# Peeling the tail of a feed-forward loop and moving a row scale behind the matmuls in a two-block transformer kernel

## The chip, the cores and the metric

The kernel runs on one core of one Trainium2 chip. The metric is the device time of one execution in microseconds (us), as the median of several runs. All times below are in us unless marked ns.

## The reference

The program computes two transformer blocks, one after the other, for one sequence of 256 tokens and a model width of 2048, in float32. Cut to what the change touches:

```
first block:   x = x + gt1 * (merged @ w_out)
               h = modulate(rms_norm(x, g_ffn), sh2, sc2)
               a = causal_dwconv(h @ w_gate, conv_w, conv_b)        # hidden width 5632
               y = (silu(a) * (h @ w_up)) @ w_down
               x = x + gt2 * y
               x = rms_norm(x, g_final)
second block:  h = rms_norm(x, norm_g)                              # EPS = 1e-6 in both norms
               q, k, v, r, a_lr = split(h @ gla_w_in)               # gated linear attention
               x = x + gla(...) @ gla_w_out
               g, u = split(rms_norm(x, norm_g2) @ w_gu)
               x = x + (silu(g) * u) @ w_down
```

`gt2` is a row of 2048 numbers made from `c @ w_ada`. Between the two blocks stand two RMS norms in a row, `g_final` and `norm_g`, and each needs the mean square of whole token rows.

## The kernel before, in words

**Tiling.** The 256 tokens are two blocks of 128 partitions (`TB = 2`). Every large product streams its weight through a ring of four 1 MB slabs (`raw`): 512 rows by 512 columns, read by the DMA queue of SyncE (SP). A slab is two halves. For each half ScalarE (ACT) rounds the weight into `whi`, VectorE (DVE) makes the remainder `wlo = raw - whi`, and TensorE (PE) does 12 matmuls of 128x512: two row tiles by two token blocks by three products (hi*hi, lo*hi, hi*lo). This stands in `split` on ACT and DVE and in `half` on PE. The ring holds four halves, so `split` of half n waits until PE has used half n-4, and ACT and DVE run at most four halves ahead of PE.

**Order.** Each engine's program is one list, written out by hand. `body(it, phase, per, hooks)` walks over the halves, calls `split` for each, and after half idx runs the steps that `hooks` has for idx. Whatever a step waits for holds up all later splits of that engine. A group of halves accumulates into one of two pairs of PSUM banks, `lin[0]` and `lin[1]` (one bank for each token block), which alternate; ACT drains token block 0 and counts `free0`, DVE drains block 1 and counts `free1`.

**The feed-forward part.** The hidden width 5632 is 11 blocks of 512 (`FB = 11`). Phase `F1p` makes gate and up of block 0 (16 halves). Phase `F1` is a hardware loop over ten iterations of 24 halves: gate of block j+1 (8), down of block j (8: four output column blocks c of 2 halves each), up of block j+1 (8). PE transposes the up values at idx 1 (`turn_up`) and the gate values at idx 9 (`turn_gate`); DVE does the convolution (`conv`, after splits 14 and 16), `activate` (18) and `hidden` (5), which makes `hid_hi` and `hid_lo`, the operand of the down product. The results of each down block are added to `yacc`: token block 1 by DVE, block 0 through `dstage` by GpSimd (POOL). Phase `F1e` is the down product of block 10 alone (8 halves). PE has nothing else to do there, so it waits for `turn_up` and `hidden`. During `F1e` the row `gt_row` is made (`modulation_row(1)`, from PE's `ada_rows(3)`), and `combine` adds `yacc * gt_row` to X, one column block after the other.

**Between the blocks.** After the last `combine`, DVE makes `xs = X * gfin` (2 instructions of 128x2048), ACT sums the squares of X and xs (4 of 128x2048), DVE and ACT form the scale `ry` of each token, xs is multiplied by it, PE transposes xs (`first_features`, then four more turns inside the first group of phase `GQ`), ACT multiplies by the column `g_n0` into `aff`, and DVE makes `act_hi` and `act_lo`. Meanwhile POOL scales X itself in place with `rstd` and `gfin`. Phases `GQ`, `GV`, `GR` then read these features. Phases `F2p`, `F2`, `F2e` of the second block have the same form as F1, without convolution and without `gt_row`; their result is added to X directly and written out in four DMAs.

Of the kernel before, what the change touches and what calls it, by code (L numbers as in the profile page):

```python
# [33 lines left out]
GL_ITEMS = (1, 2, 0, 3, 4, 5, 6)  # L34

# [4 lines left out]
    ("F1p", 1, 16, 2), ("F1", FB - 1, 24, 6), ("F1e", 1, 8, 4),  # L40
    ("GQ", 2, 16, 2), ("GV", 2, 16, 2), ("GR", 2, 16, 2), ("GO", 2, 16, 2),
    ("F2p", 1, 16, 2), ("F2", FB - 1, 24, 6), ("F2e", 1, 8, 4),
# [11 lines left out]
for _n in range(108):  # L54
    _at = 4 + _n if _n < 64 else 8 + _n if _n < 96 else 20 + _n if _n < 102 else (124, 125, 126, 126, 127, 127)[_n - 102]
    CHUNKS_AT.setdefault(_at, []).append(_n)
# [7 lines left out]
def build_program(nc, A, out):  # L64
# [68 lines left out]
    dstage = at("dstage", [P, 2, NB], ARENA + 65 * KB)  # L133

# [11 lines left out]
    alrT = at("alrT", [GR, S], ARENA + 44 * KB)  # L146
    wa2 = at("wa2", [GR, GH * GK], CONST + 10 * KB + 512)
# [27 lines left out]
    par3 = at("par3", [P, 96], CONST + 6 * KB)  # L175
# [31 lines left out]
    conv_w1, conv_w2, gla_b = par3[:, 0:44], par3[:, 44:88], par3[:, 88:96]  # L207
# [32 lines left out]
    def _(sp):  # L240
# [8 lines left out]
        def ada_chunk(n, kt=None, half=None):  # L249
# [16 lines left out]
            (2, 0, rows(A["conv_w"][0, 1])), (2, 44, rows(A["conv_w"][0, 2])), (2, 88, rows(A["gla_b_a_2"][0])),  # L266
        ]
# [56 lines left out]
        def ffn(n):  # L324
# [46 lines left out]
        for c in range(4):  # L371
            sp.wait_ge(free1, 2 + G0["F2e"] + c + 1)
            sp.wait_ge(sem("dstage_free"), 2 + 4 * (2 * FB - 1) + c + 1)
# [4 lines left out]
    def _(pe):  # L378
# [14 lines left out]
        def group(it, phase, per, gper, idx0, gi, n, hooks, kt0=0, x_hi=hi, x_lo=lo, lead=None, parts=None):  # L393
# [4 lines left out]
            for i in range(n):  # L398
# [6 lines left out]
                if lead is not None and i < 4:  # L405
                    turn(lead, 4 + i)
# [39 lines left out]
        pe.wait_ge(sem("par_in"), 13 * 16)  # L446
        for n, rws in enumerate((112, 120, 96)):
# [172 lines left out]
        def ffn(n):  # L620
# [16 lines left out]
            def turn_gate(j):  # L637
                g = G0[name + "p"] + (3 if isinstance(j, int) else 6 * j - 1)
# [25 lines left out]
            with pe.Fori(0, FB - 1) as it:  # L664
# [4 lines left out]
            turn_up(FB - 1)  # L669

            def rows_now(idx):

                if idx == 1 and n == 0:
                    pe.wait_ge(sem("gpad_made"), FB)
                    ada_rows(3)
            down(0, name + "e", 8, 4, 0, 0, FB - 1, rows_now)
# [5 lines left out]
        pe.wait_ge(sem("gt_made"), 2)  # L682


        pe.wait_ge(sem("xs_made"), 6)
        first_features(xs)
# [15 lines left out]

        def turn_block(b):
# [10 lines left out]
        group(0, "GQ", 16, 2, 0, 0, 8, none, lead=xs)  # L714
        project_ranks()
        group(0, "GQ", 16, 2, 8, 1, 8, lambda idx: turn_block(0) if idx == 13 else None)
# [86 lines left out]
        pe.wait_ge(sem("xs_made"), 8)  # L803
# [5 lines left out]
    def _(act):  # L809
        pairs, affine, squared = [0], [0], [0]  # L810
# [44 lines left out]

        def features(phase, plain, scale=None, shift=None):
# [170 lines left out]
        def ffn(n):  # L1027
# [20 lines left out]
            def sigmoid(j):  # L1048
# [3 lines left out]
                else:  # L1052
                    g = G0[name + "p"] + (3 if isinstance(j, int) else 6 * j - 1)
# [24 lines left out]
            with act.Fori(0, FB - 1) as it:  # L1078
                body(it, name, 24, hooks(it, name, 6, it + 1, 27))
            hid_high(FB - 1)  # L1080
            hk = {5 + 2 * c - (c == 3 and n == 0): [lambda c=c: down(0, name + "e", 4, c, c, 2 * c + 2)] for c in range(4)}
            if n == 0:
                body(0, name + "e", 8, hk)
            else:

                for idx in range(4, 8):
                    split(0, name + "e", 8, idx)
                    for step in hk.get(idx, ()):
                        step()
                for idx in (9, 11):  # L1090
                    hk[idx][0]()
# [865 lines left out]
```

## Time and profile before

| what | value |
|---|---|
| median of 3 runs | 2992.65 us (2988.68 to 2993.77) |
| the profiled execution, its own time | 2992.77 us |
| its span in the trace | 2990.8 us |
| PE busy (matmul) | 2749.4 us, 92% of the span |
| DVE busy | 1850.3 us, 62% |
| ACT busy | 1291.7 us, 43% |
| POOL busy | 303.6 us, 10% |
| DMA | 585.39 MB, mean 196 GB/s |

The span is the time from the first to the last instruction of the trace; the run's own time is 2.0 us longer. "Busy" is the union of an engine's instructions. The granted clock of PE is shown per stretch as a share of full speed: 1.00 is 2.4 GHz and 0.50 is 1.2 GHz. Phase F1 ends and phase GQ begins at about 1665 to 1767 us in the span, F2e at 2954 us.

### The profile page before, as it was taken

To read this page: it belongs to the slowest core of one execution; us is meant where nothing else is said; L and a number is where in the kernel's file an instruction comes from. 1 tells how busy PE (TensorE), PEld (TensorE's weight loads), DVE (VectorE), ACT (ScalarE), POOL (GpSimd) and SP (SyncE) were. 2 spreads that over 40 slices of the span, in tenths; PEclk is the share of its full clock that TensorE was granted. 3 is DMA by queue.
4 is the path that set the end of the run, shared out by engine and by line. 5 is a ranking of instruction groups with operands and counts; after the bars stand their busy time and mean duration, and the time that the engine had idled before them with its cause. 6 is when DMAs were issued, how large, how long until landed. Compare 5 with 4: busy or idle time off the path is not lost. (4 is left out here: it accounts for less than half of the span.)

```text
span 2990.8 us, 34105 instructions
## 1 busy us (share of the span) xinstructions
PE 2749.4 (92%) x12279; PEld 2248.6 (75%) x12279; DVE 1850.3 (62%) x1936; ACT 1291.7 (43%) x1505; POOL 303.6 (10%) x214
## 2 busy tenths in 40 slices
PE   0699999999998999999999679998989999999998
PEld 0587888777787788888887567785678888888886
DVE  7656776677766666666666664557545555555554
ACT  1334554345444444444444343443344444444443
POOL 0000000100010111111111330004000111111112
PEclk9989999999999999999999889998999999999999
DMA  9667776656856766666555425551054555555553
GB/s 393 239 217 247 253 254 241 231 191 216 298 170 209 248 201 199 196 201 201 198 187 195 136 93 174 170 189 65 30 195 155 193 187 196 185 194 189 189 189 120
DMA packets 266917, 585.39 MB, mean 196 GB/s; under 512 B 14300, under 2 KB 16676, under 8 KB 263900
## 3 DMA queue, kind: packets, MB, share of 16 engines
q1 hardware_dynamic: 266844, 584.41, 57.6%
q8 instruction: 46, 0.75, 0.1%
q14 instruction: 27, 0.22, 0.0%
HBM read 582.26 MB, written 2.11 MB: 195 GB/s over the span
## 5 line engine op out<-in xcount | busy, mean ns | idle before, releaser
L1205 DVE TENSOR_TENSOR sb_wlo<-sb_raw,sb_whi 128x1024 fp32r<-128x1024 f32 x896 | 1106.4, 1237 | 940.3 <-ACT sb_whi L817 940.0
L817 ACT ACTIVATE sb_whi<-sb_raw 128x1024 fp32r<-128x1024 f32 x896 | 948.1, 1060 | 1416.6 <-PE lin L390 1290.6
L388 PE MATMUL lin<-sb_whi,sb_act_hi 128*128 128x512 f32 x2880 | 1147.9, 399 | 43.1 <-DVE sb_act_lo L1267 12.8
L389 PE MATMUL lin<-sb_wlo,sb_act_hi 128*128 128x512 f32 x2880 | 1131.7, 393 | 0.0
L390 PE MATMUL lin<-sb_whi,sb_act_lo 128*128 128x512 f32 x2880 | 1131.6, 393 | 0.0
L388 PEld LDWEIGHTS lin<-sb_whi,sb_act_hi 128*128 128x128 f32 x2880 | 548.1, 190 | 164.6 <-DVE sb_wlo L1205 25.2
L390 PEld LDWEIGHTS lin<-sb_whi,sb_act_lo 128*128 128x128 f32 x2880 | 547.1, 190 | 116.6
L389 PEld LDWEIGHTS lin<-sb_wlo,sb_act_hi 128*128 128x128 f32 x2880 | 548.2, 190 | 110.9 <-issue 0.2
L388 PE MATMUL lin<-sb_whi,sb_hid_hi 128*128 128x512 f32 x704 | 278.7, 396 | 6.3 <-DVE sb_hid_lo L1504 3.7
L389 PE MATMUL lin<-sb_wlo,sb_hid_hi 128*128 128x512 f32 x704 | 276.1, 392 | 0.0
L390 PE MATMUL lin<-sb_whi,sb_hid_lo 128*128 128x512 f32 x704 | 275.8, 392 | 0.0
L388 PEld LDWEIGHTS lin<-sb_whi,sb_hid_hi 128*128 128x128 f32 x704 | 133.4, 190 | 37.8 <-DVE sb_hid_lo L1504 4.1
L390 PEld LDWEIGHTS lin<-sb_whi,sb_hid_lo 128*128 128x128 f32 x704 | 133.4, 190 | 28.0
L389 PEld LDWEIGHTS lin<-sb_wlo,sb_hid_hi 128*128 128x128 f32 x704 | 133.5, 190 | 27.4 <-issue 0.2
L1849 POOL TENSOR_TENSOR sb_yacc<-sb_yacc,sb_dstage 128x512 f32<-128x512 f32 x44 | 83.4, 1894 | 691.1 <-ACT sb_dstage L831 691.1
L1849 POOL TENSOR_TENSOR sb_x<-sb_x,sb_dstage 128x512 f32<-128x512 f32 x44 | 76.9, 1748 | 397.4 <-ACT sb_dstage L831 397.4
L1222 DVE SCALAR_TENSOR_TENSOR sb_ada_acc<-sb_ada_in,sb_small,sb_ada_acc 128x1024 f32<-128x1024 f32 x90 | 114.9, 1279 | 0.0
L451 PE MATMUL aux<-sb_onehot,sb_relb 32*8 32x512 f32 x2 | 1.9, 1036 | 87.0 <-DMA sb_relb<-in_rel_bias_dram 87.0
L1291 DVE SCALAR_TENSOR_TENSOR sb_acc<-sb_ada,sb_small,sb_acc 128x4096 f32<-128x4096 f32 x16 | 71.7, 4483 | 4.6 <-DMA sb_ada<-in_w_ada_dram 3.8
L451 PEld LDWEIGHTS aux<-sb_onehot,sb_relb 32*8 32x8 f32 x2 | 0.1, 86 | 87.4 <-DMA sb_relb<-in_rel_bias_dram 87.4
L1524 DVE SCALAR_TENSOR_TENSOR sb_cacc<-sb_gpad,sb_par,sb_cacc 128x256 f32<-128x256 f32 x88 | 58.5, 706 | 6.1 <-DVE sb_cacc L1524 1.6
L418 PE MATMUL aux<-sb_con,sb_xs 128*128 128x128 f32 x96 | 17.7, 342 | 44.1 <-issue 35.6
(294 smaller groups left out, 1628.2 us busy)
## 6 DMA issues: line engine op xcount, KB each, us to landing
sb_raw<-in_w_in_dram SPq DMA_DIRECT2D x88, 1024.0 KB, 6.2
sb_raw<-in_ffn_w_gu_dram SPq DMA_DIRECT2D x88, 1024.0 KB, 5.0
sb_ada_in<-in_w_ada_dram SPq DMA_DIRECT2D x128, 512.0 KB, 4.0
sb_raw<-in_gla_w_in_dram SPq DMA_DIRECT2D x48, 1024.0 KB, 5.1
sb_raw<-in_w_gate_dram SPq DMA_DIRECT2D x44, 1024.0 KB, 5.2
sb_raw<-in_w_up_dram SPq DMA_DIRECT2D x44, 1024.0 KB, 5.2
sb_raw<-in_w_down_dram SPq DMA_DIRECT2D x44, 1024.0 KB, 5.1
sb_raw<-in_ffn_w_down_dram SPq DMA_DIRECT2D x44, 1024.0 KB, 5.0
```

The costliest lines, as they stand in the source:

```text
L388: pe.matmul(o, x_hi[:, kt + q, t], whi[:, w], start=first and q == 0, stop=False)
L389: pe.matmul(o, x_hi[:, kt + q, t], wlo[:, w], start=False, stop=False)
L390: m = pe.matmul(o, x_lo[:, kt + q, t], whi[:, w], start=False, stop=last and q == 1)
L418: m = pe.transpose(aux[n % 4][:, q * S + tb * P:q * S + (tb + 1) * P], src[:, tb, (2 * g + q) * P:(2 * g + q + 1) * P], ident)
L451: pe.matmul(aux[3][0:NH, :], relb[:], onehot[:], start=True, stop=True).then_inc(sem("erow_T"), 1)
L817: act.activation(whi[:, idx % RING * HALF:(idx % RING + 1) * HALF], raw[:, idx // 2 % RING, idx % 2 * HALF:(idx % 2 + 1) * HALF], ACT.Copy ...
L1205: dve.tensor_tensor(wlo[:, c], raw[:, idx // 2 % RING, idx % 2 * HALF:(idx % 2 + 1) * HALF], whi[:, c].bitcast(fp32), ALU.subtract).then_i ...
L1222: dve.scalar_tensor_tensor(acc[:, c], ada_in[:, half, :], cact[:, ds(kt, 1)], acc[:, c], ALU.mult, ALU.add).then_inc(sem("ada_sum"), 1)
L1291: dve.scalar_tensor_tensor(acc0[:], ada0[:, u, :], cact[:, ds(4 * it + u, 1)], acc0[:], ALU.mult, ALU.add).then_inc(sem("ada0_sum"), 1)
L1524: m = dve.scalar_tensor_tensor(cacc[:, f, :], gpad[:, f, 2 - k:2 - k + S], col(w, f), cacc[:, f, :], ALU.mult, ALU.add)
L1849: pool.tensor_tensor(y[:, 0, s], y[:, 0, s], dstage[:, c % 2, :], ALU.add).then_inc(sem("dstage_free"), 1)
```

## The change

1. In both feed-forward parts the loop does nine iterations instead of ten. Its last block is written out as one phase of 32 halves (`F1e`, `F2e`): gate of block 10, up of block 10, and then 16 halves of down, for block 9 (b=0) and block 10 (b=1) in the order `TAIL`. For each output column block c, both hidden blocks accumulate in one PSUM group. Block 10 has operand tiles of its own, `hid2_hi` and `hid2_lo`.
2. In F1e, `ada_rows(3)` comes after half 5 and `modulation_row(1)` after split 9. What the loop has summed in `yacc` goes into X in the middle of the tail (`early_sum` on DVE, `combine` on POOL). The last two blocks go into X from PSUM, one column block at a time, for both token blocks on DVE (`finish(c)`: lin*gt_row, then + X; in F2e one instruction for each token block).
3. The features of GQ are transposed from X itself, without any token scale. Four of the eight pairs are turned inside F1e after halves 24 to 27, four inside GQ. ACT multiplies by the column `g_n0 * g_fin` straight from PSUM and DVE subtracts (`scaled_pair`). The token scale `ry` is applied when GQ, GV and GR are drained from PSUM, and to the 16 rank columns through two small matmuls (`spread_scale`).
4. Squares are summed per column block on ACT (16 of 128x512), X * gfin is made in place by POOL (8 of 128x512), and the final scale of X is on ACT (`final_x`, 4 of 128x1024).
5. 110 instead of 108 chunks of `w_ada` are read ahead of the loop: the ones from 96 on start four slabs earlier, and the last four slabs of F1p carry seven instead of six. One small parameter load (`g_final`) is added at the start.

The core of the diff:

```diff
+TAIL = ((0, 0), (1, 0), (0, 1), (1, 1), (2, 0), (3, 0), (2, 1), (3, 1))
-    ("F1p", 1, 16, 2), ("F1", FB - 1, 24, 6), ("F1e", 1, 8, 4),
+    ("F1p", 1, 16, 2), ("F1", FB - 2, 24, 6), ("F1e", 1, 32, 6),
...
@@ PE
-            turn_up(FB - 1)
-            down(0, name + "e", 8, 4, 0, 0, FB - 1, rows_now)
+            for k in range(2):
+                group(0, name + "e", 32, 6, 8 * k, k, 8, at_end)
+            for s, (c, b) in enumerate(TAIL):
+                if b == 0:
+                    pe.wait_ge(free0, G0[name + "e"] + 2 + c + 1)
+                    pe.wait_ge(free1, G0[name + "e"] + 2 + c + 1)
+                pe.wait_ge(sem("hid_made"), base + FB - 1 + b)
+                for i in range(2):
+                    half(0, name + "e", 32, 16 + 2 * s + i, 2 + c, 2 * i, b == 0 and i == 0, b == 1 and i == 1,
+                         hid2_hi if b else hid_hi, hid2_lo if b else hid_lo)
+                    at_end(16 + 2 * s + i)
+            def at_end(idx):
+                if idx == 1:
+                    turn_up(FB - 2)
+                if idx == 5 and n == 0:
+                    ada_rows(3)
+                if idx == 9 and n == 0:
+                    turn_gate(FB - 1)
+                if idx == 16:
+                    turn_up(FB - 1)
+                if idx in range(24, 28) and n == 0:
+                    turn(X, idx - 24, (sem("x_made"), (idx - 24) // 2 + 1))
...
-        pe.wait_ge(sem("xs_made"), 6)
-        first_features(xs)
-        group(0, "GQ", 16, 2, 0, 0, 8, none, lead=xs)
+        group(0, "GQ", 16, 2, 0, 0, 8, none, lead=X, ready=sem("x_made"))
@@ DVE, tail of F1
+            hk = hooks(0, name + "e", 6, FB - 1, 19)
+            add(5, lambda: hidden(FB - 2))
+            add(21, lambda: hidden(FB - 1, hid2_hi, hid2_lo))
+            for c, idx in enumerate((25, 27, 33, 35)):
+                add(idx, lambda c=c: finish(c))
+                add(9, lambda: modulation_row(1))
+                for c, idx in enumerate((12, 13, 15, 17)):
+                    add(idx, lambda c=c: early_sum(c))
+                for g in range(4):
+                    add(28 + g, lambda g=g: scaled_pair(g, g_n0))
@@ POOL
-            for c in range(4):
-                down(0, name + "e", 4, c, c)
+                for c in range(4):
+                    combine(y, c, 1, c == 3)
-            link(pool.tensor_scalar(X[:, tb, :], X[:, tb, :], rstd[:, tb:tb + 1], None, ALU.mult))
-            m = pool.tensor_tensor(X[:, tb, :], X[:, tb, :], gfin[:], ALU.mult)
```

**DVE in the tail of F1.** The first piece is DVE's list of before, from the end of the loop to the first column blocks of X (`wlo` is a split, `yacc<-yacc,lin` the drain of a down block, `yacc<-yacc,gt_row` and `x<-x,yacc` a `combine`):

```order
L1500 TENSOR_TENSOR sb_hidf<-aux,sb_cacc 128x512 x2
L1504 TENSOR_TENSOR sb_hid_lo<-sb_hidf,sb_hid_hi 128x1024
L1205 TENSOR_TENSOR sb_wlo<-sb_raw,sb_whi 128x1024 x2
L1545 TENSOR_TENSOR sb_yacc<-sb_yacc,lin 128x512
L1205 TENSOR_TENSOR sb_wlo<-sb_raw,sb_whi 128x1024
L1459 TENSOR_TENSOR sb_gt_row<-aux,sb_gt_bias 128x512 x4
L1205 TENSOR_TENSOR sb_wlo<-sb_raw,sb_whi 128x1024
L1545 TENSOR_TENSOR sb_yacc<-sb_yacc,lin 128x512
L1469 TENSOR_TENSOR sb_yacc<-sb_yacc,sb_gt_row 128x512
L1470 TENSOR_TENSOR sb_x<-sb_x,sb_yacc 128x512
```

The second is the changed list around splits 15 to 21 of the new F1e (`cacc<-gpad` is the convolution, `cacc<-cacc,csig` is `activate`, `ubuf<-lin` the drain that `turn_up` needs):

```order
L1276 TENSOR_TENSOR sb_wlo<-sb_raw,sb_whi 128x1024
L1557 TENSOR_TENSOR sb_yacc<-sb_yacc,sb_gt_row 128x512
L1558 TENSOR_TENSOR sb_x<-sb_x,sb_yacc 128x512
L1276 TENSOR_TENSOR sb_wlo<-sb_raw,sb_whi 128x1024
L1607 TENSOR_SCALAR sb_cacc<-sb_gpad,sb_par_131,sb_par_130 128x256 x2
L1612 SCALAR_TENSOR_TENSOR sb_cacc<-sb_gpad,sb_par_131,sb_cacc 128x256 x2
L1612 SCALAR_TENSOR_TENSOR sb_cacc<-sb_gpad,sb_par_130,sb_cacc 128x256 x2
L1276 TENSOR_TENSOR sb_wlo<-sb_raw,sb_whi 128x1024
L1557 TENSOR_TENSOR sb_yacc<-sb_yacc,sb_gt_row 128x512
L1558 TENSOR_TENSOR sb_x<-sb_x,sb_yacc 128x512
L1276 TENSOR_TENSOR sb_wlo<-sb_raw,sb_whi 128x1024
L1619 TENSOR_TENSOR sb_cacc<-sb_cacc,sb_csig 128x1024
```

The `combine` work has moved from behind all matmuls to between the splits of the tail, ahead of the steps that make the last hidden block.

**PE between the blocks.** Before, PE's list at the seam reads as follows (`lin<-whi,hid_hi` are the last down matmuls, `aux<-con,xs` the transposes of the finished features):

```order
L388 MATMUL lin<-sb_whi,sb_hid_hi 128x512
L389 MATMUL lin<-sb_wlo,sb_hid_hi 128x512
L390 MATMUL lin<-sb_whi,sb_hid_lo 128x512
L418 MATMUL aux<-sb_con,sb_xs 128x128 x16
L388 MATMUL lin<-sb_whi,sb_act_hi 128x512
```

In the changed program transposes of X stand between down matmuls, after half 24 of F1e:

```order
L399 MATMUL lin<-sb_whi,sb_hid_hi 128x512
L400 MATMUL lin<-sb_wlo,sb_hid_hi 128x512
L401 MATMUL lin<-sb_whi,sb_hid_lo 128x512
L429 MATMUL aux<-sb_con,sb_x 128x128 x4
L399 MATMUL lin<-sb_whi,sb_hid_hi 128x512
```

Sixteen transposes that stood in one block behind the last down matmul are now four pieces of four with down matmuls between them, and their source is X instead of xs.

## Rows read from the trace of the kernel before

**Rows 1.** Windows: us; busy of PE, PEld, DVE, ACT, POOL; PEclk, DMA share, GB/s

```profile
1727.30:1740.00 12.70, 6.13 (x22) 5.41 (x23) 12.30 (x5) 2.82 (x7) 12.62 (x3) 0.63 0.00 1
```

**Rows 2.** Timeline of PE, F1 to GQ: start, us, engine, line, what, [idle before <-releaser]

```profile
1668.33 1.25 PE L633 MATMUL aux<-sb_con,sb_ubuf 128*128 128x128 f32 x8 [3.05 <-issue]
1673.31 0.79 PE L388 MATMUL lin<-sb_whi,sb_hid_hi 128*128 128x512 f32 x1 [3.73 <-DVE sb_hid_lo L1504]
1681.70 3.59 PE L440 MATMUL aux<-sb_ada_acc,sb_con 128*128 128x512 f32 x8
1684.73 0.79 PE L388 MATMUL lin<-sb_whi,sb_hid_hi 128*128 128x512 f32 x1
...
1727.40 3.45 PE L418 MATMUL aux<-sb_con,sb_xs 128*128 128x128 f32 x16 [25.77 <-issue]
1737.32 0.77 PE L388 MATMUL lin<-sb_whi,sb_act_hi 128*128 128x512 f32 x1 [6.47 <-DVE sb_act_lo L1267]
...
1755.40 0.60 PE L418 MATMUL aux<-sb_con,sb_xs 128*128 128x128 f32 x4
1755.76 0.47 PE L388 MATMUL lin<-sb_whi,sb_act_hi 128*128 128x512 f32 x1
...
1766.74 0.28 PE L692 MATMUL aux<-sb_act_hi,sb_alr_hi 128*16 128x256 f32 x1
```

**Rows 3.** Timeline of ACT at the end of the last loop iteration of F1

```profile
1665.32 1.06 ACT L817 ACTIVATE sb_whi<-sb_raw 128x1024 fp32r<-128x1024 f32 x1 [1.66 <-PE lin L390]
1670.94 1.06 ACT L1035 ACTIVATE sb_hid_hi<-sb_hidf 128x1024 fp32r<-128x1024 f32 x1 [4.08 <-DVE sb_hidf L1500]
```

**Rows 4.** Timeline of DVE with POOL idle: convolution, split, drain, hidden, gt_row

```profile
963.38 0.73 DVE L1519 TENSOR_SCALAR sb_cacc<-sb_gpad,sb_par,sb_par 128x256 f32<-128x256 f32 x2
964.15 1.80 DVE L1524 SCALAR_TENSOR_TENSOR sb_cacc<-sb_gpad,sb_par,sb_cacc 128x256 f32<-128x256 f32 x4
...
1666.41 1.22 DVE L1205 TENSOR_TENSOR sb_wlo<-sb_raw,sb_whi 128x1024 fp32r<-128x1024 f32 x1 [1.49 <-ACT sb_whi L817]
1667.55 0.68 DVE L1240 COPY sb_ubuf<-lin 128x512 f32<-128x512 f32 x1
1669.62 1.29 DVE L1500 TENSOR_TENSOR sb_hidf<-aux,sb_cacc 128x512 f32<-128x512 f32 x2 [1.39 <-PE aux L633]
1672.03 1.23 DVE L1504 TENSOR_TENSOR sb_hid_lo<-sb_hidf,sb_hid_hi 128x1024 fp32r<-128x1024 f32 x1 [1.12 <-ACT sb_hid_hi L1035]
...
1690.36 2.48 DVE L1459 TENSOR_TENSOR sb_gt_row<-aux,sb_gt_bias 128x512 f32<-128x512 f32 x4
```

**Rows 5.** Timeline of DVE and POOL, both at work on SBUF

```profile
1700.82 4.50 DVE L1205 TENSOR_TENSOR sb_wlo<-sb_raw,sb_whi 128x1024 fp32r<-128x1024 f32 x2
1704.32 2.13 POOL L1828 TENSOR_TENSOR sb_yacc<-sb_yacc,sb_gt_row 128x512 f32<-128x512 f32 x1
1705.96 1.04 DVE L1469 TENSOR_TENSOR sb_yacc<-sb_yacc,sb_gt_row 128x512 f32<-128x512 f32 x1
1706.52 1.59 POOL L1829 TENSOR_TENSOR sb_x<-sb_x,sb_yacc 128x512 f32<-128x512 f32 x1
1707.03 1.63 DVE L1470 TENSOR_TENSOR sb_x<-sb_x,sb_yacc 128x512 f32<-128x512 f32 x1
```

**Rows 6.** Timeline of PE after a short wait in the F1 loop

```profile
1643.23 0.49 PE L388 MATMUL lin<-sb_whi,sb_act_hi 128*128 128x512 f32 x1 [0.90 <-DVE sb_yacc L1545]
```

**Rows 7.** Timeline of the end of F2, all engines

```profile
2955.70 1.74 POOL L1855 TENSOR_TENSOR sb_ubuf<-sb_ubuf,sb_cacc 128x512 f32<-128x512 f32 x1 [19.99 <-ACT sb_ubuf L831]
2957.49 1.09 PE L633 MATMUL aux<-sb_con,sb_ubuf 128*128 128x128 f32 x8 [3.53 <-POOL sb_ubuf L1855]
2961.16 0.80 PE L388 MATMUL lin<-sb_whi,sb_hid_hi 128*128 128x512 f32 x1 [2.57 <-DVE sb_hid_lo L1508]
2985.14 0.39 PE L390 MATMUL lin<-sb_whi,sb_hid_lo 128*128 128x512 f32 x1
...
2986.30 1.26 POOL L1849 TENSOR_TENSOR sb_x<-sb_x,sb_dstage 128x512 f32<-128x512 f32 x1 [4.15 <-ACT sb_dstage L831]
```

**Rows 8.** Timeline of SP's DMA issues at the start

```profile
6.37 0.40 SPq L270 DMA_DIRECT2D sb_x<-in_x_dram  x1
```

More of the change, by code:

```diff
@@ L53 @@
 CHUNKS_AT = {}
-for _n in range(108):
-    _at = 4 + _n if _n < 64 else 8 + _n if _n < 96 else 20 + _n if _n < 102 else (124, 125, 126, 126, 127, 127)[_n - 102]
+for _n in range(110):
+    _at = 4 + _n if _n < 64 else 8 + _n if _n < 96 else 16 + _n if _n < 103 else (124, 124, 125, 126, 126, 127, 127)[_n - 103]
     CHUNKS_AT.setdefault(_at, []).append(_n)
@@ L701, in gq_hooks, with spread_scale @@
             return run
+        def spread_scale():
+            pe.wait_ge(sem("rdiag_made"), 1)
+            for tb in range(TB):
+                m = pe.matmul(aux[1][0:GR, tb * P:(tb + 1) * P], ones[:, 0:GR], rdiag[:, tb, :], start=True, stop=True)
+            m.then_inc(sem("rrow_T"), 1)
         def turn_block(b):
@@ L854, in norm_rows, with scaled_pair @@
             act.activation(dst[:, 0, :], X[:, 0, :], ACT.Copy, scale=rstd[:, 0:1]).then_inc(sem("xs_made"), 1)
+        def scaled_pair(g, col):
+            n = pairs[0]
+            act.wait_ge(sem("tt_T"), n + 1)
+            for q in range(2):
+                kt = 2 * g + q
+                m = act.activation(hi[:, kt, :], aux[n % 4][:, q * S:(q + 1) * S], ACT.Copy, scale=col[:, kt:kt + 1])
+            m.then_inc(sem("tt_hi"), 1)
+            pairs[0] += 1
         def features(phase, plain, scale=None, shift=None):
@@ L1572, in ffn, with early_sum @@
[L1572 to L1591 removed]
+            def early_sum(c):
+                dve.wait_ge(free1, 2 + G0["F1e"])
+                combine(y, c, False, c == 3)
@@ new lines, in finish @@
+            def finish(c):
+                drained(0, name + "e", (22, 24, 30, 32)[c])
+                s = slice(c * NB, (c + 1) * NB)
+                for tb, free in ((0, free0), (1, free1)):
+                    if n:
+                        dve.tensor_tensor(X[:, tb, s], X[:, tb, s], lin[c % 2][tb][:], ALU.add).then_inc(free, 1)
+                    else:
+                        dve.tensor_tensor(y[:, tb, s], lin[c % 2][tb][:], gt_row[:, s], ALU.mult).then_inc(free, 1)
+                for tb, free in ((0, free0), (1, free1)) if n == 0 else ():
+                    dve.wait_ge(free, 2 + G0[name + "e"] + 2 + c + 1)
+                    m = dve.tensor_tensor(X[:, tb, s], X[:, tb, s], y[:, tb, s], ALU.add)
+                if n == 0:
+                    m.then_inc(sem("x_made"), 1)
```

283 lines of the change are left out of this document (168 added, 115 removed).

## The prediction

> **What bounds the kernel now.** I began with the page: TensorE (PE) is busy in nearly the whole span, so only time in which PE stands still or runs at the low clock can be won. The waits of PE, stretch by stretch, then show where that is, and two places belong to the change. In the timeline of PE at the end of the first feed-forward part [rows 2] the reader sees four waits: 3.05 for the last up block, 3.73 for the hidden block, 25.77 while X, its squares and the token scale are made, and 6.47 for the first features. They sum to 39.0. The second place is the end of F2 [rows 7], with 3.53 and 2.57.
>
> The waits cost more than their length. After the long one PE ran at a granted clock of 0.63 [rows 1], near the lower level of 1.2 GHz. The first two halves after the 3.73 took 1681.70-1673.31 = 8.4 [rows 2], where two halves at full speed take 5.4: one half is 1.06+1.66 = 2.72, read from ScalarE's splits, which PE paces [rows 3]. So a wait of that kind costs some 3.0 on top in F1.
>
> **What stands still before.** The last half of the loop ended at 1668.33-3.05 = 1665.3, and the first GQ group at 1766.74 [rows 2]: 101.5. PE's necessary work in it is 16 halves (43.5), `ada_rows` (1684.73-1681.70 = 3.0), eight turns at 1755.76-1755.40 = 0.36 (2.9) and `turn_up`, two turns' worth (0.7): 50.1. So 51.4 are lost. In F2 the stretch runs from 2957.49-3.53 = 2954.0 to 2985.1 [rows 7] = 31.2; its eight halves (21.5 to the start of the last matmul) and `turn_up` (0.7) leave 9.0 lost.
>
> **The change part by part: F1.** PE's own work is the same, plus two tiny matmuls for the rank scale (0.3, an estimate from the 128x256 rank matmul's 0.28 [rows 2]). The waits depend on whether VectorE (DVE) keeps up in the tail, since six kinds of work now stand between its splits. I count from T, the start of half 6, behind `ada_rows`. DVE prices without GpSimd [rows 4]: split 1.14 between starts (1667.55-1666.41), drain 0.68, `gt_row` 2.48, one `conv` 0.77+1.72 = 2.5, hidden 1.29+1.23. `activate` is of the split's shape, 1.14. While GpSimd (POOL) runs `combine`, a split takes 2.25, the product with `gt_row` 1.04 and the addition to X 1.63 [rows 5]; without POOL I take half a split, 0.7, for each of the last two. A split can start when the half four before it is used, about 1.3 later on DVE.
>
> - Split 9 is done before T. `gt_row` runs T+0.2 to 2.7, and POOL begins four times product and addition: 2.13+1.59 = 3.7 each [rows 5], so until T+17.6.
> - Split 10 ends at 6.3, split 11 at 9.0, the gate drain at 9.6, split 12 at 11.9, the first `early_sum` (2.9) at 14.8, split 13 at 17.1. POOL has cost DVE 4 x 1.1 + 1.3 = 5.7. PE begins half 12 at 17.0 (6 x 2.72 and `turn_gate` 0.7), so all these are in time.
> - Second `early_sum` to 18.6, split 14 19.8, `conv` 22.3, split 15 23.5 (PE needs it at 25.2), third `early_sum` 24.9, split 16 26.1, `conv` 28.6, split 17 29.8, fourth `early_sum` 31.2, split 18 32.4, `activate` 33.5, split 19 34.7, drain of up 35.4. With the short hand-overs between them I put it at T+35.8.
> - PE ends half 16 at T+11 x 2.72+0.7 = 30.6 and wants this drain for `turn_up`: a wait of 5.2. It is of the length of those that brought the clock down, so I add 2.5 for half 17 (the lower of the two prices, since in F2 the loss is 31.2-22.2-3.53-2.57 = 2.9 with the slow `turn_up`) and 0.4 for `turn_up`.
> - `hidden` of block 10 stands behind split 21: 2.5 after half 17, then 1.29, 1.06 on ScalarE [rows 3] and 1.23, with hand-overs 6.2. The two halves of c=1, b=0 cover 5.4: a wait of 0.8.
>
> The new F1 tail loses 5.2+2.5+0.4+0.8 = 8.9.
>
> **The seam to GQ.** From T', the start of half 30: split 33 and `finish(2)` (two drains 0.7 each, two additions 0.7 each, hand-overs) are done at 5.6; ScalarE's squares of c=2 hold its split 35 until 8.6, so `finish(3)` ends at about 13.5 with POOL beside it. PE wants c=2 at 8.2, c=3 at 14.3: covered by 2.6 and 0.8. The last feature pair and split are due on DVE at 25.2, PE comes at 25.9. The margins are 0.7 to 0.8; I charge 1.0 for them. The token scale is late without harm: POOL's last product ends near 21.8, squares and root near 27, and the first GQ drain comes after 28.6; behind it PE still has 5.6 of rank matmuls, and the other PSUM pair is free. If this cover were gone, the drain would hold both split queues. The final scale of X (four halves of rows on ScalarE) and the scaled drains lie beside GQ's halves, where ScalarE is idle 1.66 of 2.72 [rows 3].
>
> F1 gains 51.4+0.9 (one loop iteration fewer with its wait [rows 6]) -8.9-1.0-0.3 = 42.1.
>
> **F2.** `turn_up` now waits for POOL's product at 3.53 behind the last up half, and half 16 covers 2.72 of it: 0.8 stay. After a wait of 0.90 the first matmul took 0.49 and the next was at full speed [rows 6], so no clock is lost. ScalarE and DVE make the hidden block before the two halves of c=1 are over. So 9.0 become 0.8. At the very end two DVE additions (0.68 each, [rows 4]) follow the last matmul, where a drain and POOL's addition ended 2986.30+1.26-2985.53 = 2.0 after it [rows 7]: 0.6 more. F2 gains 8.8.
>
> **Rest.** One more issue on the sync queue ahead of the first loads, 0.45 [rows 8]. The `w_ada` chunks moved ahead of the loop lie beside halves of U and F1p with DVE idle 1.49 before a split [rows 4]; I take 0, and 1 as the upper end.
>
> **Sum.** 42.1+8.8-0.5 = 50.4. The profiled execution's own time is 2992.77, within 0.2 of the median, so 2992.8-50.4 = **2942.4**.
>
> **A rule weighed.** DVE and POOL slow each other: two splits took 4.50 beside POOL [rows 5]. The Trainium skill, "SBUF — State Buffer", section "SBUF: two separate sides", says more: the port pair that DVE and GpSimd share is an exclusive lock held for a whole instruction. By that rule each of POOL's eight instructions blocks DVE for all its length.
>
> **The rivals.**
> - POOL blocks DVE by its full length: eight instructions at 1.26, POOL's price alone [rows 7], are 10.1 instead of 5.7, and the up drain comes 4.4 later: 2946.8. For it: the 4.50. Against: POOL too is stretched (2.13), so there are pauses in which DVE runs. Chance 0.17. It is what the rule of the Trainium skill's page "SBUF — State Buffer" would give.
> - DVE keeps up: early sums and POOL finish sooner than I add up, PE waits only for the structure (0.4 at `turn_up`, since the drain comes 2.5+0.6 after half 15 and half 16 covers 2.72, and 0.8 at the hidden block), the clock stays up and the seam costs nothing: 7.7+1.0 better, 2933.7. Against it stand nearly 36 of DVE work before 30.6 of PE work. Chance 0.15.
> - The seam is not closed: with margins under 1, POOL's eight products beside the splits, or the squares ahead of the splits on ScalarE, leave waits of 3 to 5 each at c=3 and at the last pairs, one with the low clock behind it: 10 to 17 more, 2952 to 2959. Chance 0.16.
> - Slower: the clock. If the waits of the tail left PE at 1.2 GHz from half 17 on, a half would cost 2.4 more. From 21 halves on that eats the gain, and through GQ (47 halves) it is +113: about 3055. For it: the granted clock of 0.63 [rows 1]. Against: after the 3.73 full speed was back within two halves [rows 2]. Chance 0.03.
> - The change frees nothing, because X or the scale is awaited at the new places just as long: within 0.2% (6, about what a measurement of this kernel tells from no change). That would need PE to wait 50 more in a stretch whose producers I find at most some microseconds late. Chance 0.02.
>
> **How the numbers follow.** The forecast itself has 0.47, with a range of its own of 2938 to 2947 (DVE's table wrong by 3 either way, and the clock price there or not). Leaving out the slower case and the far end of the open seam, the range is 2932 to 2957. Faster 0.95, same 0.02, slower 0.03.
>
> **What the new profile would show.** The 25.77 and the 6.47 are gone from PE's waits; one wait of 3 to 8 stands before the `turn_up` of F1e with a fall of the granted clock behind it, one under 1 before the first `hid2` half; in F2 one wait near 0.8 before `turn_up`. Wrong would be: no wait at `turn_up` (DVE's prices too high), a long wait at the turns of X or at the GQ splits (the seam), or a stretch of GQ at half clock.

## The result and the profile after

| what | before | after |
|---|---|---|
| median (4 runs each) | 2992.88 us (2988.68 to 2993.77) | 2938.98 us (2934.87 to 2941.72) |
| ratio to before | | 0.9826 (0.9814 to 0.9839) |
| profiled execution, its span | 2990.8 us | 2939.9 us (the run's own time 2941.72) |

Before was measured once more for this comparison, so that its median now has four runs. The changed kernel is 53.9 us faster by the medians and 50.9 by the spans; 50.4 was forecast.

The page of the changed kernel, its first part: busy time of each engine, share of the span, instructions.

```profile
PE 2740.4 (93%) x12283; PEld 2240.5 (76%) x12283; DVE 1826.7 (62%) x1948; ACT 1287.5 (44%) x1514; POOL 267.6 (9%) x202
```

PE's busy time fell by only 9.0 (from 2749.4); fewer of its matmuls ran at the low clock. The other 42 are idle time that is gone.

**The end of F1.** The timeline of PE in the changed kernel from the last loop iteration to the ranks, the counterpart of [rows 2, 6]:

```profile
1575.21 0.49 PE L399 MATMUL lin<-sb_whi,sb_act_hi 128*128 128x512 f32 x1 [0.89 <-DVE sb_yacc L1633]
...
1653.24 1.21 PE L644 MATMUL aux<-sb_con,sb_ubuf 128*128 128x128 f32 x8 [4.45 <-issue]
...
1654.67 0.63 PE L400 MATMUL lin<-sb_wlo,sb_hid_hi 128*128 128x512 f32 x1
...
1657.23 0.49 PE L400 MATMUL lin<-sb_wlo,sb_hid_hi 128*128 128x512 f32 x1
...
1664.68 0.50 PE L399 MATMUL lin<-sb_whi,sb_hid_hi 128*128 128x512 f32 x1 [0.56 <-DVE sb_hid_lo L1592]
...
1681.67 0.60 PE L429 MATMUL aux<-sb_con,sb_x 128*128 128x128 f32 x4
1684.87 0.60 PE L429 MATMUL aux<-sb_con,sb_x 128*128 128x128 f32 x4
...
1801.23 1.22 PE L760 MATMUL aux<-sb_alrT,sb_wa 16*128 16x256 f32 x2 [2.46 <-DVE sb_gu L1750]
```

The waits of 25.77 and 6.47 have no counterpart. Two are left up to GQ, 4.45 for the last up block and 0.56 for the hidden block. The 2.46 at L760, behind GQ, is no work of the change: before, the same matmul waited 2.40. After the 4.45, a matmul takes 0.63 instead of 0.39 until 1657.2; the windows of the changed kernel (columns as in [rows 1]) show the same fall, and a seam without a gap:

```profile
1652.00:1660.00 8.00, 6.76 (x27) 5.65 (x28) 2.42 (x4) 1.06 (x1) 0.00 (x0) 0.79 0.45 144
1680.00:1720.00 40.00, 40.00 (x191) 33.03 (x191) 30.11 (x43) 29.57 (x59) 16.12 (x10) 1.00 0.53 177
```

**What DVE does ahead of the up drain.** The timeline of DVE in the tail of the changed kernel, with three of POOL's rows; they answer to [rows 4, 5]:

```profile
1618.05 2.48 DVE L1547 TENSOR_TENSOR sb_gt_row<-aux,sb_gt_bias 128x512 f32<-128x512 f32 x4 [1.11 <-PE aux L451]
...
1632.22 2.31 DVE L1276 TENSOR_TENSOR sb_wlo<-sb_raw,sb_whi 128x1024 fp32r<-128x1024 f32 x1
1634.46 1.78 DVE L1557 TENSOR_TENSOR sb_yacc<-sb_yacc,sb_gt_row 128x512 f32<-128x512 f32 x1
1636.27 0.69 DVE L1558 TENSOR_TENSOR sb_x<-sb_x,sb_yacc 128x512 f32<-128x512 f32 x1
1636.88 1.22 DVE L1276 TENSOR_TENSOR sb_wlo<-sb_raw,sb_whi 128x1024 fp32r<-128x1024 f32 x1
...
1652.45 0.68 DVE L1312 COPY sb_ubuf<-lin 128x512 f32<-128x512 f32 x1
1653.05 1.22 DVE L1276 TENSOR_TENSOR sb_wlo<-sb_raw,sb_whi 128x1024 fp32r<-128x1024 f32 x1
1659.84 1.23 DVE L1276 TENSOR_TENSOR sb_wlo<-sb_raw,sb_whi 128x1024 fp32r<-128x1024 f32 x1 [5.58 <-ACT sb_whi L852]
```
```profile
1620.68 1.30 POOL L1952 TENSOR_TENSOR sb_yacc<-sb_yacc,sb_gt_row 128x512 f32<-128x512 f32 x1 [41.14 <-DVE sb_gt_row L1547]
...
1631.71 1.75 POOL L1952 TENSOR_TENSOR sb_yacc<-sb_yacc,sb_gt_row 128x512 f32<-128x512 f32 x1
1633.54 2.16 POOL L1953 TENSOR_TENSOR sb_x<-sb_x,sb_yacc 128x512 f32<-128x512 f32 x1
```

Until POOL stops at 1635.70, a split takes up to 2.31 and an operation of a sum up to 1.78; behind that they take 1.22 and 0.69. And one split behind the up drain, for which PE waits, DVE itself stands idle for 5.58.

The rows also show how the two engines share. They take turns, one whole instruction each: POOL's product ends at 1633.46, the split that DVE had started in its middle ends at 1634.53, 1.07 later, POOL's next operation at 1635.70, 1.17 later, and DVE's product at 1636.24, 0.54 later. Each time this is about what the instruction takes alone (1.14 between the starts of two splits, 1.29 for POOL, 0.6 between two DVE operations of 128x512).

**The end of F2.** The timeline of the changed kernel, first PE, then DVE, the counterpart of [rows 7]:

```profile
2893.44 1.09 PE L644 MATMUL aux<-sb_con,sb_ubuf 128*128 128x128 f32 x8 [0.89 <-POOL sb_ubuf L1979]
...
2894.60 0.39 PE L400 MATMUL lin<-sb_wlo,sb_hid_hi 128*128 128x512 f32 x1
...
2934.97 0.39 PE L401 MATMUL lin<-sb_whi,sb_hid_lo 128*128 128x512 f32 x1
```
```profile
2935.40 1.28 DVE L1671 TENSOR_TENSOR sb_x<-sb_x,lin 128x512 f32<-128x512 f32 x2 [4.15 <-PE lin L401]
```

One wait of 0.89 stays, the clock keeps its level behind it, and nothing waits for the hidden block.

**A wait that grew.** The waits of PE in the changed kernel, grouped (line, what for: us in total, times, longest):

```profile
PE lin L399 <- DVE sb_wlo L1276: 13.7, 3, 8.3
```

The longest of the three stands at the first matmul of the F1 loop; the same wait was 6.15 before. In the timeline of PE:

```profile
978.38 0.79 PE L399 MATMUL lin<-sb_whi,sb_act_hi 128*128 128x512 f32 x1 [8.25 <-DVE sb_wlo L1276]
```

**Where the 50.9 of the spans lie**, read by the same instruction in both timelines of PE: the stretches ahead of F1 gave 2.0 (not the change, see the last experiment); F1p with the first loop iteration cost 2.4 (108.40 from the turns of xs, PE's transposes of the features ahead of F1p, to the `yacc` wait at 1027.27, before 105.98); from the `yacc` wait of the last common iteration (1575.21, before 1574.76) to the awaited matmul of the ranks' product at L760 (1801.23, before 1843.99) 226.02 instead of 269.23, so 43.2; F2's tail 8.5. These sum to 51.3; stages in between differ by some tenths.

### The profile page after: what moved, and what is told of

Read it like the earlier page. It is cut to its first block, busy times and chain, and to the rows that moved or that the text cites. A ratio compares the mean times of both kernels' runs of the same rounds, so it can differ in the third digit from the quotient of the medians.

```text
span 2939.9 us, 33831 instructions
## 1 busy us (share of the span) xinstructions
PE 2740.4 (93%) x12283; PEld 2240.5 (76%) x12283; DVE 1826.7 (62%) x1948; ACT 1287.5 (44%) x1514; POOL 267.6 (9%) x202
## 4 chain that ended last, share of the span: by engine, by line
PE 84%; DVE 6%; issue 3%; ACT 2%; DMA 1%; DVEq 0%; POOL 0%; SPq 0%; POOLq 0%; ACTq 0%
PE lin L399 26%; PE lin L401 26%; PE lin L400 26%; DVE sb_wlo L1276 2%; DVE sb_cacc L1612 1%; ACT sb_whi L852 1%; PE aux L429 1%; PE aux L821 1%; PE aux L644 1%; PE aux L787 1%; DVE sb_cacc L1607 0%; DMA sb_raw<-in_w_gate_dram 0%; DVE sb_yacc L1633 0%; DVE sb_gm L1815 0%; PE aux L655 0%
## 5 line engine op out<-in xcount | busy, mean ns | idle before, releaser
L1973 POOL TENSOR_TENSOR sb_yacc<-sb_yacc,sb_dstage 128x512 f32<-128x512 f32 x36 | 68.3, 1898 | 596.6 <-ACT sb_dstage L866 596.6
L1973 POOL TENSOR_TENSOR sb_x<-sb_x,sb_dstage 128x512 f32<-128x512 f32 x36 | 63.7, 1770 | 336.1 <-ACT sb_dstage L866 336.1
L1899 POOL COPY sb_st_sb<-sb_sbz 128x768 f32 (+1 forms) x8 | 7.5, 942 | 422.4 <-DVE sb_sbz L1312 274.5
```

The lines of the kernel that those rows point to most:

```text
L1973: pool.tensor_tensor(y[:, 0, s], y[:, 0, s], dstage[:, c % 2, :], ALU.add).then_inc(sem("dstage_free"), 1)
```

## The experiments

Edits are against the changed kernel. Since unchanged stages differ by some us from run to run, I compare two stretches of PE's timeline beside the times: **S1** from the turns of xs to the `yacc` wait in the first loop iteration (108.4 in the changed kernel), and **S2** from the `yacc` wait of the last loop iteration to L760 (226.0). All runs of before that stood beside them had medians of 2988.6 to 2991.8.

### The peeled tails with the old seam

The deferred scale is undone: turns of xs only after X, squares of whole rows, scaled copy and unscaled drains; the tails stay peeled. The core of it on ACT:

```diff
-        for g in range(4, 8):
-            scaled_pair(g, g_n0)
...
+        act.wait_ge(sem("x_made"), 4)
+        squares(X, ss)
+        act.wait_ge(sem("xy_made"), 2)
+        squares(xs, ssy)
...
+        features("GQ", False, g_n0)
```

> The tails stay peeled, the seam to GQ goes back to its old form (X complete, squares of whole rows, scaled copy xs, turns and split pairs only then). Theory A: the deferred scale brings most of the gain. The second tail keeps its gain of about 8.5 us, the first tail alone brings about nothing (its old waits of 3.05 and 3.73 us against the new 4.45 us with its low clock), and the wait at the seam is back at 20 to 26 us with the low clock behind it: 2975 to 2986 us. Rival B: the peeled tail brings half or more of the first gain, because X is complete sooner: seam wait below 15 us, 2950 to 2962 us.

Measured: 2968.39 us (2965.78 to 2970.1), ratio 0.9924 (0.9908 to 0.9941). Its PE timeline:

```profile
1653.41 1.94 PE L644 MATMUL aux<-sb_con,sb_ubuf 128*128 128x128 f32 x8 [4.39 <-issue]
...
1715.40 3.68 PE L429 MATMUL aux<-sb_con,sb_xs 128*128 128x128 f32 x16 [17.01 <-ACT sb_xs L1161]
1725.38 0.77 PE L399 MATMUL lin<-sb_whi,sb_act_hi 128*128 128x512 f32 x1 [6.29 <-DVE sb_act_lo L1339]
```

Neither range held. The direction is A's: S2 is 256.8, so the deferred scale is worth 30.8 and the peeled first tail 12.4 of the 43.2. The 30.8 are those of the whole set that this edit undoes (scale, squares by column block, early turns), not of the scale alone. But the tail brings more than "about nothing", and the larger part of the reason is in the first wait of the seam: 17.01 instead of 25.77. ACT's timeline in this kernel, first row, and in before, second row, shows where most of the 8.8 come from:

```profile
1703.24 1.91 ACT L878 ACTIVATE sb_junk<-sb_x 128x2048 f32<-128x2048 f32 x1 [2.17 <-DVE sb_x L1660]
```
```profile
1714.24 1.91 ACT L843 ACTIVATE sb_junk<-sb_x 128x2048 f32<-128x2048 f32 x1 [9.46 <-DVE sb_x L1470]
```

The squares start 4.85 after PE has stopped (1715.40-17.01 = 1698.39), where they started 12.61 after it before (1727.40-25.77 = 1701.63): 7.8 of the 8.8. With the loop's sum already in X, only one column block's product and addition stand behind the last matmul; before, DVE still had its sums and splits beside POOL to do, and ACT waited 9.46 for X.

### VectorE's early sums behind the up drain

```diff
-                for c, idx in enumerate((12, 13, 15, 17)):
+                for c, idx in enumerate((20, 20, 23, 29)):
```

> VectorE's four early sums of the first tail stand behind the up drain (three there or near it, the last between the later drains), in the idle stretch of 5.6 us that it has there; nothing else changes. Theory A (VectorE's queue ahead of the up drain is too full): the wait of 4.45 us before the up turn falls below 1 us, the clock stays at 1.00 there, and the stretch is 5 to 7 us shorter: 2932 to 2934 us. Rival B (GpSimd's eight operations at the shared memory, which stay where they were, cause the delay by themselves): the wait stays at 3 us or more. Rival C: the sums only move the wait, and the one for the hidden block's low part grows by 3 us or more.

Measured: 2936.24 us (2931.72 to 2938.79), ratio 0.9814 (0.9798 to 0.983). PE's timeline, and the windows of PE alone (us, PE busy, PEclk, DMA share, GB/s):

```profile
1652.52 1.06 PE L644 MATMUL aux<-sb_con,sb_ubuf 128*128 128x128 f32 x8 [0.40 <-issue]
1662.36 0.50 PE L399 MATMUL lin<-sb_whi,sb_hid_hi 128*128 128x512 f32 x1 [0.59 <-DVE sb_hid_lo L1592]
```
```profile
1652.00:1660.00 8.00, 7.60 (x38) 1.00 0.45 139
```

A: the wait is 0.40, the clock stays, the hidden block is as before, and S2 is 220.4, 5.6 shorter. The wait accounts for 4.05 of that, so the low clock and the slow `turn_up` had cost 1.6. The expected total (2932 to 2934) was missed; the profiled execution was 3.4 later at 1575 already, ahead of the edit. Two of the four sums stand in the 5.58 in which DVE was idle, the other two behind later splits.

### GpSimd's combinations behind the up drain

```diff
                 pool.wait_ge(sem("dstage_free"), 2 + 4 * (FB - 2))
+                pool.wait_ge(free1, 2 + G0["F1e"] + 2)
```

> GpSimd's four combinations of the first tail wait until VectorE has drained up; VectorE's own order is unchanged. Theory A (VectorE loses 5.4 us to GpSimd beside it and 5.6 us to its own sums): VectorE's operations ahead of the up drain run at 0.68 and 1.23 us each, and the wait of 4.45 us before the up turn falls below 0.7 us with the clock kept; the slowdown goes to the operations behind it (the hidden block's low part and the first finishing sums), which cost 0 to 3 us: 2932 to 2937 us. Rival B (GpSimd's time is not VectorE's loss): the wait stays at 3 us or more. Rival C (the combinations end too late): a new wait of more than 2 us before the third down group, 2940 us or more.

Measured: 2937.09 us (2936.36 to 2937.88), ratio 0.982 (0.9804 to 0.9837). PE's timeline, and two rows of DVE's:

```profile
1654.85 1.06 PE L644 MATMUL aux<-sb_con,sb_ubuf 128*128 128x128 f32 x8 [1.23 <-issue]
```
```profile
1633.27 0.68 DVE L1557 TENSOR_TENSOR sb_yacc<-sb_yacc,sb_gt_row 128x512 f32<-128x512 f32 x1
...
1664.56 6.78 DVE L1276 TENSOR_TENSOR sb_wlo<-sb_raw,sb_whi 128x1024 fp32r<-128x1024 f32 x3
```

The wait falls from 4.45 to 1.23, above the 0.7 of A and far below the 3 of B; the clock stays; S2 is 221.2 (4.8 shorter). With POOL away the sums run at 0.68. The slowdown has moved to three later splits (6.78, 2.26 each), where it costs PE nothing. So POOL's neighbourhood is 3.2 of the wait. Moving either the sums or POOL is nearly enough, because each alone puts DVE's list below PE's time.

### The up turn one half later

```diff
-                if idx == 16:
+                if idx == 17:
                     turn_up(FB - 1)
```

> In both tails TensorE turns the last up block one half later (1.7 us of matmuls go first). Theory A: the wait in the first tail falls from 4.45 to 2.5 to 2.9 us, that in the second from 0.89 us to nothing, and the wait for the hidden block's low part grows from 0.56 to 0.6 to 2 us: 2936 to 2939 us; the clock still falls in the first, since a wait of over 2 us is left. Rival B: the later turn is given back in full by the wait for the hidden block: 2939 to 2942 us.

Measured: 2933.65 us (2933.3 to 2936.23), ratio 0.9812 (0.9796 to 0.9829). PE's timeline and window:

```profile
1653.35 1.06 PE L644 MATMUL aux<-sb_con,sb_ubuf 128*128 128x128 f32 x8 [1.68 <-issue]
```
```profile
1652.00:1660.00 8.00, 6.65 (x34) 1.00 0.80 275
```

Better than A said: the wait is shorter by the whole half (2.77; the expectation took 1.7 for a half, which is 2.72), no wait for the hidden block is left, and after a wait of 1.68 the clock is still 1.00, so S2 is 220.7, 5.3 shorter. In F2 the wait of 0.89 is gone as expected.

### One slice behind each slab

```diff
-... 16 + _n if _n < 103 else (124, 124, 125, 126, 126, 127, 127)[_n - 103]
+... 16 + _n if _n < 106 else (124, 125, 126, 127)[_n - 106]
```

> The last seven slices of the modulation weights, of which the change puts two behind each of two slabs at the end of the first FFN block, go one behind each slab. Theory A (the wait of 8.25 us at the loop's first matmul, 6.15 us before the change, has grown by the doubled slices): it falls to 5 to 6.5 us and the stretch from the turns of the first FFN to the end of its loop is 2 to 3 us shorter. Rival B: other loads ahead of those slabs set it, and the wait stays within 0.7 us of 8.25 us.

Three of the last seven slices thus go to slabs 119 to 121, and the last four slabs carry four instead of seven (six before the change).

Measured: 2933.82 us (2933.45 to 2936.39), ratio 0.9817 (0.9795 to 0.9839). S1 is 101.6, 6.8 shorter: more than the growth that the change had brought, and more than A said. The wait at the loop's first matmul falls from 8.25 to 2.13, below A's 5 to 6.5:

```profile
973.59 0.50 PE L399 MATMUL lin<-sb_whi,sb_act_hi 128*128 128x512 f32 x1 [2.13 <-DVE sb_wlo L1276]
```

SP's issues in the changed kernel, and in this one:

```profile
947.96 0.44 SPq L251 DMA_DIRECT2D sb_raw<-in_w_up_dram  x1
948.78 4.39 SPq L262 DMA_DIRECT2D sb_ada_in<-in_w_ada_dram  x2
953.22 0.43 SPq L251 DMA_DIRECT2D sb_raw<-in_w_up_dram  x1
958.79 1.52 SPq L262 DMA_DIRECT2D sb_ada_in<-in_w_ada_dram  x2
960.36 0.43 SPq L348 DMA_DIRECT2D sb_gt_bias<-in_b_ada_dram  x1
...
962.57 8.35 SPq L251 DMA_DIRECT2D sb_raw<-in_w_gate_dram  x1
```
```profile
953.48 0.34 SPq L262 DMA_DIRECT2D sb_ada_in<-in_w_ada_dram  x1
953.86 0.43 SPq L348 DMA_DIRECT2D sb_gt_bias<-in_b_ada_dram  x1
...
956.15 10.35 SPq L251 DMA_DIRECT2D sb_raw<-in_w_gate_dram  x1
```

A pair of slices holds the queue, here for 4.39, because the second needs a buffer that DVE has yet to add up. The slabs behind them are late, ACT's splits too, and with them the additions that free the next buffers. One by one, the first gate slab's issue begins 6.4 sooner in the trace, and 8.5 sooner after the turns of xs (920.94 here, 918.87 there). Part of this is given back at once: the issue itself, right behind the four small loads, lasts 10.35 instead of 8.35, and nothing that the trace names releases it. The next slab follows 0.3 behind it (966.75 against 971.19), 6.5 sooner after the turns of xs, which is about the gain of S1.

### The four loads behind the loop

The lines `sp.dma_start(gt_bias...)`, `gfin`, `gn` and `alr_raw` with their wait stand ahead of `gate_up(0, name + "e", ...)` instead of ahead of the loop.

> The four broadcast and small loads (the bias of the gate row, g_final, the gate norm, the raw rank weights) go behind the first FFN's loop instead of ahead of its first gate slabs. Theory A (these rows stand in the queue ahead of the gate slabs and share their transfer): the wait of 8.25 us falls below 4 us: 5 to 8 us shorter there, 2932 to 2936 us. Rival B: the wait is of the modulation slices alone and stays above 7 us. Rival C: the loads are late at their new place, and VectorE's sum of the gate row, or TensorE's fifth half in the tail behind it, waits by more than 3 us: no gain or a loss.

Measured: 2936.51 us (2935.54 to 2938.05), ratio 0.9828 (0.9806 to 0.985). S1 is 100.7, 7.7 shorter, so A; S2 is 226.7 with the same two waits (4.45 and 0.56), so nothing waits for the loads at the new place. ACT's timeline, the first gate split of the loop in the changed kernel and in this one:

```profile
976.01 2.00 ACT L852 ACTIVATE sb_whi<-sb_raw 128x1024 fp32r<-128x1024 f32 x2 [12.88 <-DMA sb_raw<-in_w_gate_dram]
```
```profile
968.31 2.01 ACT L852 ACTIVATE sb_whi<-sb_raw 128x1024 fp32r<-128x1024 f32 x2 [4.29 <-DMA sb_raw<-in_w_gate_dram]
```

The four loads carry 1024, 1024, 256 and 128 KB ahead of the slab that PE needs next. Without them SP's issue of that slab takes 0.39 instead of 8.35:

```profile
961.54 0.39 SPq L251 DMA_DIRECT2D sb_raw<-in_w_gate_dram  x1
```

With them gone the wait of 8.25 becomes three of 0.27, 0.51 and 0.60, although the pairs of slices are still there. Each of the two edits takes most of the wait; it needs both, a late queue and 2.4 MB in front of the slab. Why the issue behind the loads lasts 8 to 10 is not shown.

### The early turns after the tail

Turns 0 to 3 of X after halves 28 to 31 instead of 24 to 27, their scaled pairs behind splits 32 to 35; the scale stays deferred.

> The scale stays deferred, but the first four turns of X come four halves later (after the last four halves of the tail) and their scaled pairs behind the tail's last splits. Theory A (with the scale out of the way only the last block's drain, one turn and one split pair stand behind the last matmul, and the early turns hide the rest): TensorE then waits at the first GQ halves for pairs that are made late, 4 to 8 us in all: 2943 to 2947 us. Rival B: the early turns bring nothing on top of the deferred scale: within 1 us of the changed kernel in the stretch from the tail's last up turn to the ranks.

Measured: 2947.14 us (2944.89 to 2948.82), ratio 0.9862 (0.9839 to 0.9884); S2 230.2, 4.2 longer. PE's timeline:

```profile
1702.81 0.47 PE L399 MATMUL lin<-sb_whi,sb_act_hi 128*128 128x512 f32 x1 [1.28 <-DVE sb_yacc L1673]
...
1714.45 0.63 PE L429 MATMUL aux<-sb_con,sb_x 128*128 128x128 f32 x4 [2.24 <-DVE sb_x L1676]
```

A, at its lower end. The two waits, 3.5 in sum, are most of the 4.2. So of the 30.8 some 4 come from turning the first columns early, the other 27 from the rest of what the old seam undid: the scale and the squares no longer stand between X and the turns.

### All four together

Sums, turn, slices and loads as above in one kernel.

> Together: VectorE's sums behind the up drain, the up turn one half later, one slice behind each slab, the four loads behind the loop. If each finding holds and they do not meet: no wait over 0.6 us in the first tail, the wait at the loop's first matmul below 4 us, the second tail without its 0.89 us: 12 to 16 us below the changed kernel, 2923 to 2927 us. Rival: the loads and the tail's slabs meet, and one of the gains is given back: 2929 to 2934 us.

Measured: 2922.65 us (2918.84 to 2926.1), ratio 0.9783 (0.9758 to 0.9808). S1 97.0, S2 219.9. That is 16.3 below the changed kernel's first median, at the edge of the 12 to 16 expected. No wait is left at the loop's first matmul or at the up turns; the one for the hidden block is 0.73, a little over the 0.6. It was run again, beside the changed kernel on one chip:

> The changed kernel once more, unaltered, beside the combined version on one chip. It gives the spread that the stages ahead of the change have from run to run (so far the stretch up to 600 us differed by up to 5.6 us between kernels that are the same there) and the time that the combination is held against: 2936 to 2942 us, with waits of 8.2 us (the loop's first matmul), 4.4 us (up turn of the first tail) and 0.9 us (second tail).

> The combined version once more. If its gain is that of the waits (about 11.4 us in the first block and the loop's first iteration, 6.1 us in the first tail, 0.9 us in the second), it is 15 to 19 us below the changed kernel on the same chip: 2919 to 2925 us. Rival: the first look was a good draw, and the difference is 8 to 13 us.

Measured: the changed kernel 2943.73 us (2937.98 to 2944.97), ratio 0.9839 (0.9825 to 0.9852), above the 2936 to 2942 expected, with waits of 8.57, 4.45 and 0.89; the combination **2920.12 us** (2919.05 to 2923.32), ratio 0.9768 (0.9755 to 0.9781), so 23.6 less. The spans are 2943.2 and 2917.2. Of these 26.0, S1 gives 11.0 (108.3 to 97.3), S2 6.0 and the part from the turns of F2's xs to the end 1.1: 18.1, inside the 15 to 19 expected of the waits. The time's difference is above that range, because another 7.9 lie in stages that are the same in both. At a matmul ahead of the whole change the two timelines read:

```profile
595.95 0.79 PE L399 MATMUL lin<-sb_whi,sb_act_hi 128*128 128x512 f32 x1 [4.18 <-DVEq L1472]
```
```profile
589.75 0.79 PE L399 MATMUL lin<-sb_whi,sb_act_hi 128*128 128x512 f32 x1 [4.19 <-DVEq L1472]
```

The first profile of the changed kernel had 590.39 there. The windows of the two executions, columns as in [rows 1], show where half of the 6.2 arises:

```profile
575.00:582.00 7.00, 7.00 (x23) 5.82 (x23) 0.08 (x1) 0.00 (x0) 0.00 (x0) 0.52 0.00 0
575.00:582.00 7.00, 7.00 (x35) 5.54 (x35) 3.06 (x3) 2.60 (x4) 0.00 (x0) 1.00 0.00 0
```

PE waits in neither. In the first, the granted clock falls at 575.2, in the middle of 32 small transposes, and is back at 581.7; in the second it stays up, and 3.2 of the 6.2 come from this. The executions fall into two groups by it: those with 1.00 in this window pass the matmul at 589.8 to 591.0, those with 0.52 to 0.63, the kernel before among them, at 594.3 to 596.2. What decides between the two is not shown. So 4 to 6 us of a comparison of two executions of this kernel can come from there, and differences of that size were read from stretches, not from times.

## Why the prediction was right, point by point

- **F1p and the slices** (0, upper end 1): wrong. It cost 2.4. The step that failed is that the chunks "lie beside halves of U and F1p with DVE idle": it asked whether DVE has time for the additions, and not what a slice that waits for its buffer holds up in SP's queue. The runs show the queue, and 2.4 MB of loads in it, as the cause: taking either away shortened S1 by 6.8 and 7.7.
- **The up drain at T+35.8**: measured. `gt_row` starts at 1618.05, which the forecast called T+0.2, so T is 1617.85, and the drain ends at 1653.13, T+35.3; PE stopped at 1653.24-4.45 = 1648.79, T+30.9 (forecast 30.6). (PE's own record of half 6 starts at 1617.39, which would make both 0.5 later.) The wait was 4.45 instead of 5.2.
- **POOL's cost to DVE** (5.7): the stretched operations (splits 2.06, 1.58, 2.31; sums 1.77, 1.67, 1.78) sum to 5.4 over their prices alone. But taking POOL away shortened the wait by 3.2 only, since DVE then waits for ACT between its first splits. The rival's 10.1 fell. By the Trainium skill, "SBUF — State Buffer", section "SBUF: two separate sides", the lock is held for a whole instruction, and the trace agrees: the two engines take turns (1.07, 1.17 and 0.54 from one end to the next, above). What the 10.1 had wrong is that DVE wants SBUF during all eight of POOL's instructions. During the first two it waited for ACT or had started first and lost nothing, during the fourth it lost 0.36, as most of that time went to a drain from PSUM; the other five cost it 0.84 to 1.09 each.
- **The clock price** (2.5+0.4): over-sized. 1.6 in all, by what the run with the sums moved gains beyond the wait. The low level lasted from 1654.1 to 1657.2, 3.1 instead of a whole half.
- **The hidden block's wait** (0.8): 0.56. The tail thus lost 6.6 where 8.9 were forecast.
- **The seam** (charge 1.0): no wait at all. Its margins were there, and PE is busy for 40.00 of 40.00 in 1680 to 1720. The run with late turns shows the margin as thin: four halves later, 3.5 of waits return.
- **F1 in sum**: 42.1 forecast, 43.2 measured. (Its list of four waits left out a fifth, 2.40 at 1747.92, but the 51.4 was taken from the whole stretch and holds it.) The tail and the seam came out 3.3 better, so 45.4 were to be had; about 2 went elsewhere. One part is visible: a half with a turn in it takes 1684.87-1681.67 = 3.20, so a turn costs 0.48 and not 0.36, 1.0 for eight. A second is the rank scale: from the first rank matmul (1723.12, before 1766.74) to the first one of L760 (1797.64, before 1840.46) PE takes 0.8 longer, where the forecast had 0.3 for the two small matmuls. The other 0.7 I can't place.
- **F2**: 8.8 forecast, 8.5 measured; the 0.89 wait, the kept clock and the missing hidden wait as the steps had them.
- **The clock rival** (3055): fell; full speed was back 4 us after the wait of 4.45. **Nothing freed**: fell.
- **The rest** (0.5 at the start): X's first turns came at 112.77 instead of 112.52, 0.3.
- **The sum**: the forecast of 2942.4 lies between the two medians of the changed kernel, 2938.98 and 2943.73. Its closeness to a us is partly luck, since F1p (2.4 against), the stages ahead of it (2.0 for) and F1 (1.1 for) cancel.

What the experiments added to the forecast: I had expected the peeled tail alone to be worth nothing in F1. It is worth 12.4; 7.8 of them because the loop's sum leaves the path at the seam, and 2.7 because the waits of the old tail (3.05, 3.73 and the loop's 0.90) became 4.39 and 0.58.

## What to carry to other kernels

A wait at a seam is best cut by asking what really needs the complete result: here a row scale commutes with the matmul, and moving it to the drains, with the squares and the early turns that go with it, was worth 30.8, the peeled loop 12.4 and 8.5. When steps are put into a hand-written list, place them behind the drain that the next engine waits for, where the list has its idle time, and let the consumer come one step later; either edit won back 5.3 to 5.6. Ask of every moved load what stands behind it in its queue: spare time on the engine that consumes the data says nothing about a queue that waits for a buffer.

## What the runs showed of the hardware

- DVE and POOL, both with operations on two SBUF inputs, took turns by whole instructions: a DVE split of 128x1024 went from 1.22 to as much as 2.31, an operation of 128x512 of its sums from 0.69 to 1.78, POOL's own 128x512 from 1.29 to 2.37. What POOL costs DVE is therefore its length only where DVE wants SBUF at that time: 5.4 for eight instructions of 1.26 to 1.30. DVE operations that read PSUM were not slowed: a drain took 0.68 beside POOL at 1626.6 and 0.68 without it at 1652.45.
- TensorE's granted clock was 1.00 after waits of 0.89, 1.23 and 1.68 in the tails and fell after one of 4.45. The length of the wait alone does not decide: behind the 2.46 at L760, with matmuls on 16 rows around it, the clock of the changed kernel was 0.50 from 1801 to 1810.8, and at 575.2 it fell in some executions with no wait at all. The low stretch behind L760 is in both kernels and behind the end of S2.
- SP's issue of a 1 MB slab took 8.35 and 10.35 right behind four loads of 2.4 MB, and 0.39 without them.
- Identical instructions of the stage up to 600 us took 4 to 6 us more in some executions than in others, in two groups that the clock at 575 to 582 tells apart (0.52 to 0.63, or 1.00).
